# One of eight row blocks of the modulation weights multiplied on TensorE instead of VectorE

## The reference

```python
c_act = jax.nn.silu(c)                                    # (1, 1024)
mod = (c_act @ w_ada[i] + b_ada[i])[:, None, :]           # w_ada[i] is 1024 x 6144
sh1, sc1, g1, sh2, sc2, g2 = jnp.split(mod, 6, axis=-1)
h = rms_norm(x) * (1 + sc1) + sh1                         # x is (1, 1024, 1024)
proj = h @ w_in[i]
...
```

## Time and profile before

| | |
|---|---|
| time, median of 3 runs | 2814.91 us (2812.26 to 2815.58) |
| the profiled execution's own time | 2812.64 us |
| its span | 2810.8 us (1.84 us lie around it) |
| PE (TensorE) busy | 2741.2 us, 98% |
| DVE (VectorE) busy | 1631.8 us, 58% |
| ACT (ScalarE) busy | 956.0 us, 34% |
| POOL (GpSimd) busy | 942.9 us, 34% |
| PE share of the chain that ended last | 92% |

### The profile page before, as it was taken

One profiled execution on the slowest core, in us unless ns is written; L12 is line 12 of the kernel. 1 busy time (PEld: TensorE's weight loads), 2 busy tenths in 40 slices (PEclk: granted clock), 3 DMA queues, 4 the chain that ended last, 5 costly groups with the idle time before them and its releaser, 6 DMA issues.

```text
span 2810.8 us, 60971 instructions
## 1 busy us (share of the span) xinstructions
PE 2741.2 (98%) x25491; PEld 2287.8 (81%) x25491; DVE 1631.8 (58%) x1807; ACT 956.0 (34%) x1447; POOL 942.9 (34%) x691
## 2 busy tenths in 40 slices
PE   5999999999999999999999999999999999999999
PEld 4798989898989898988787777788888788888887
DVE  4645454545454545469694666466648643333896
ACT  5312121212121212135555768301113333334343
POOL 0403030303030303034343111233333477777443
PEclk9999999999999999999999999999999999999999
DMA  5202020202020202033332111366511133234353
GB/s 211 74 22 61 21 61 21 61 21 61 21 61 21 61 21 61 11 116 115 119 112 72 34 62 50 118 196 211 173 58 45 53 113 113 85 100 142 124 170 92
DMA packets 255359, 235.00 MB, mean 84 GB/s; under 512 B 24353, under 2 KB 213883, under 8 KB 255099
## 3 DMA queue, kind: packets, MB, share of 16 engines
q1 hardware_dynamic: 241632, 183.74, 21.7%
q10 hardware_dynamic: 13467, 47.31, 4.8%
HBM read 184.08 MB, written 46.92 MB: 82 GB/s over the span
## 4 chain that ended last, share of the span: by engine, by line
PE 92%; DVE 3%; ACT 2%; issue 1%; DMA 0%; SPq 0%; POOL 0%; ACTq 0%; DVEq 0%; POOLq 0%
PE ps L306 68%; PE ps L1243 3%; PE ps L1257 3%; PE ps L1254 2%; PE ps L1221 2%; PE ps L1306 1%; PE ps L1443 1%; PE ps L1468 1%; PE ps L1211 1%; PE ps L1456 1%; PE ps L1177 1%; PE ps L1263 1%; PE ps L1290 1%; PE ps L1280 1%; PE ps L1309 1%
## 5 line engine op out<-in xcount | busy, mean ns | idle before, releaser
L306 PE MATMUL ps<-x_hi,w_hi 128*128 128x512 f32 (+1 forms) x2372 | 801.4, 397 | 6.1 <-issue 2.0
L306 PE MATMUL ps<-x_hi,w_lo 128*128 128x512 f32 (+1 forms) x2372 | 783.2, 390 | 0.0
L306 PE MATMUL ps<-x_lo,w_hi 128*128 128x512 f32 (+1 forms) x2372 | 782.9, 390 | 0.0
L296 POOL CAST w_hi<-w_raw 128x1024 fp32r<-128x1024 f32 (+2 forms) x161 | 153.5, 954 | 1544.8 <-PE ps L306 1292.2
L306 PEld LDWEIGHTS ps<-x_hi,w_hi 128*128 128x128 f32 (+1 forms) x2372 | 436.8, 187 | 114.5 <-issue 22.4
L306 PEld LDWEIGHTS ps<-x_hi,w_lo 128*128 128x128 f32 (+1 forms) x2372 | 443.9, 187 | 96.8
L306 PEld LDWEIGHTS ps<-x_lo,w_hi 128*128 128x128 f32 (+1 forms) x2372 | 444.2, 187 | 92.6
L298 POOL TENSOR_TENSOR w_lo<-w_raw,w_hi 128x1024 fp32r<-128x1024 f32 (+2 forms) x161 | 329.3, 2045 | 12.9
L306 PE MATMUL ps<-x_sums,w_hi 128*128 128x512 f32 x648 | 201.7, 392 | 0.6 <-issue 0.6
L1054 POOL TENSOR_TENSOR w_lo<-arena,w_hi 128x384 fp32r<-128x384 f32 (+1 forms) x124 | 154.6, 1248 | 111.2 <-ACT w_hi L2216 111.2
L2519 DVE COPY_PREDICATED arena<-hid,ps 128x256 f32<-128x256 int32 x144 | 72.0, 500 | 139.4 <-PE ps L1254 88.6
(11 more groups left out here) (346 smaller groups left out, 4449.2 us busy)
## 6 DMA issues: line engine op xcount, KB each, us to landing
w_raw<-in_w_in SPq DMA_DIRECT2D x78, 512.0 KB, 3.9
arena<-in_w_ada SPq DMA_DIRECT2D x48, 512.0 KB, 5.8
arena<-gates_sig ACTq DMA_DIRECT2D x40, 512.0 KB, 4.3
w_raw<-in_w_ffn_in SPq DMA_DIRECT2D x26, 512.0 KB, 4.0
gates_sig<-arena ACTq DMA_DIRECT2D x24, 512.0 KB, 2.7
under<-in_w_ffn_in SPq DMA_DIRECT2D x18, 512.0 KB, 5.7
hidden_sums<-arena SPq DMA_DIRECT2D x36, 256.0 KB, 2.6
under<-hidden_sums SPq DMA_DIRECT2D x11, 768.0 KB, 5.8
```

The lines of the kernel that those rows point to most:

```text
L296: nc.gpsimd.tensor_copy(hi, raw).then_inc(s_whi, 1)
L306: ins = nc.tensor.matmul(dst[h], wp, xp[h], start=first and m == 0, stop=last and m == 2, skip_group_check=on)
```

## The change

Piece 4 no longer goes through VectorE. Before `mod_sums` of the first half, TensorE waits for silu(c) and for the part that holds piece 4, and multiplies it by eight matmuls: stationary operand 128 columns of the raw piece, moving operand the column of silu(c). They open the accumulation in columns 0 to 7 of bank 0 of `ps`, and the eight matmuls of `mod_sums(0, 0)` now add to what stands there (`start=False`). VectorE leaves piece 4 out; so that all later counts stay as they were, piece 5 waits for the count of 4 and raises `ada_acc` by two.

```diff
+        ADA_ON_PE = (4,)
...
             def mod_sums(half, bank):
                 pe.wait_ge(ada_acc, upto(KT if half == 0 else ADA_ACC0))
+                own = half > 0
                 for c in range(KT):
-                    ins = mm(ps[:, bank, c:c + 1], ada_acc0[:, half, c * P:(c + 1) * P], ones[:, 0:1], start=True, stop=True)
+                    ins = mm(ps[:, bank, c:c + 1], ada_acc0[:, half, c * P:(c + 1) * P], ones[:, 0:1], start=own, stop=True, skip_group_check=not own)
                 ins.then_inc(ada_pe, 1)
 
+            pe.wait_ge(p0_act, upto(1))
+            for n in ADA_ON_PE:
+                part, count = ada_part(n)
+                pe.wait_ge(s_ada[part], 16 * count)
+                for c in range(KT):
+                    mm(ps[:, 0, c:c + 1], ada_w0[:, n, c * P:(c + 1) * P], mod[:, 48 + n:49 + n], start=n == ADA_ON_PE[0] and c == 0, stop=False, skip_group_check=True)
             mod_sums(0, 0)
...
                 if n in first:
                     ins = v.tensor_scalar(acc, ada_w0[:, n % ADA_SLOTS, :], c_k, None, ALU.mult)
                 else:
-                    dve.wait_ge(ada_acc, upto(n))
+                    dve.wait_ge(ada_acc, upto(4 if n == 5 else n))
                     ins = v.scalar_tensor_tensor(acc, ada_w0[:, n % ADA_SLOTS, :], c_k, acc, ALU.mult, ALU.add)
-                ins.then_inc(ada_acc, 1)
+                ins.then_inc(ada_acc, 2 if n == 5 else 1)
...
             for n in range(2, KT):
-                ada_piece(n)
+                if n not in ADA_ON_PE:
+                    ada_piece(n)
```

## The result

The changed kernel takes 2819.55 us (median of 20 runs, 2815.59 to 2821.79), the kernel before 2813.67 us in as many runs beside it (2811.49 to 2815.92). The ratio is 1.0021, with a 95% interval of 1.0014 to 1.0027: **slower by 5.9 us**, outside the range of the prediction and on the side to which it gave a chance of 0.03. The profiled execution took 2818.98 us, its span is 2817.2.

A forecast was written before the change was run, and what follows sets the result against it. TensorE was taken as the bound, busy 98% of the span, so only an earlier first dense product counts: 0.11 us off for the removed multiplication, nothing for the added rows, from 2814.91 to 2814.8 us. Range 2811.5 to 2817.0.

The forecast's parts named there:

- The added work's price of nothing: Sixteen TensorE rows from about 25.6 us, in idle time ahead of the sums, cost nothing; 1.8 to 3.6 us uncovered.
- The removed multiplication: In the opening, VectorE without piece 4 waits 1.28 us for part (5,8), so one multiplication less gains 0.11 us.
- Rival A: In the opening, TensorE at its high clock for the sums, 1.84 us not 3.58; gain 0.33 us, 2814.6; chance 0.11.
- Rival B: In the opening, part (5,8) lands before 28.4, so the whole multiplication is gained: 1.0 to 1.4 us, 2813.6; chance 0.07.
- Rival C: TensorE's low clock reaches into the first dense products: about 2.8 us slower, 2817.6; chance 0.07.
- Rival D: Part (5,8) lands 0.11 us later, VectorE starts piece 5 as before: no gain, 2814.9; chance 0.72 together with the forecast.

The follow-up runs named there:

- padded by 223: The changed kernel plus 223 unused semaphore increments in TensorE's list, everything behind lying 256 slots later than in the kernel before: ratio 1.0035.
- place 207: Loop start at slot 207 of a 256-slot block: the changed kernel +5.9 us, kernel before plus only the added matmuls +5.5, plus only 33 increments +5.8.
- 174: Loop start at slot 174 of a 256-slot block, as in the kernel before; the changed kernel with its loop set there: ratio 0.9994, 2812.65 us.
- place 238: The kernel before plus 64 unused increments in TensorE's list, loop start at slot 238 of a 256-slot block: ratio 1.0057, +15.8 us.
- 14: The changed kernel with its loop set to start at slot 14 of a 256-slot block: ratio 1.0054, 2829.13 us.
- 142: The changed kernel with its loop set to start at slot 142 of a 256-slot block: ratio 1.0016, median 2820.21 us.
- the padding of 192: The kernel before plus 192 unused increments in TensorE's list, loop start at slot 110: ratio 1.0072, +21.1 us, 6 of it in the opening.

## Why the prediction was wrong

- **The step that failed** is in its first paragraph: "a change in the opening is worth what it moves the moment at which TensorE starts its dense products, and after that moment the program follows unchanged". The instructions are unchanged, their place isn't. The padded kernel, the same except for 33 empty slots, is 5.8 us slower, and the changed kernel with its loop in the old place is not slower.
- **The added work's price of nothing** missed the same term. Its sixteen rows did run in idle time, from 27.56 for 3.54 us. Their price was 33 slots of TensorE's list, and it is paid in the loop: 4.8 us by the table. No rival named it. The profile of before held a hint that I didn't follow: pauses of TensorE with no releaser. The waits view of the kernel before, over the loop:

```profile
PE ps L1290 <- issue: 5.0, 8, 0.9
PE ps L1263 <- issue: 0.9, 4, 0.3
```

  The hint says where to look and not how much it is worth: all such pauses in the loop add up to 6.3 us before and to 6.9 after, and the 5.0 us of the first row are 4.9 after. The rest of the loop's loss is in steps that the view doesn't name and in the half clock.

- **The removed multiplication** was sized right. The reading of the landings held: part (5,8) landed 4.0 us after piece 4 in the profile after, 4.06 by the estimate. From the first multiplication of part (2,5) to the first of part (5,8) it is 4.17 us before and 4.03 to 4.05 in four of six traces without piece 4 on VectorE (a seventh, padded by 223, starts so late that all its parts have landed), a gain of 0.12 to 0.14 us for the 0.11 forecast. In the other two the part landed later, and it is 4.51 and 5.03 (waits of 1.84 and 2.36 us): a loss of 0.3 and 0.9. So the term is right for the trace that it was read from and of no fixed sign beyond it. The gain can't be seen in any ratio; 0.9994 and 1.000 allow it and don't show it.
- **Rival A** fell: the sums took 3.58 us in the changed kernel too. **Rival B** fell: the wait was there in each trace of the change except the one padded by 223. **Rival C** had the right sign for a wrong reason: the first products ran at full pace, 12 rows in 3.02 us. **Rival D** can't be told from the forecast by the ratio; the two late landings are of its kind.
- **The range** was built of the spread of executions of one program. Three runs at one place of the loop could not contain what another place does.
- **The half clock** is a second term that the prediction had at nothing behind the opening. By the granted clock of each run (mean 0.99895 over the 20 of the changed kernel, 0.99926 over 31 of the kernel before) it is, as an estimate, 0.0003 x 2817 = 0.9 us of the 5.9. Whether the change has to do with it is not shown; the two runs with the place 207 and without the whole change have 0.99856 and 0.99873.

The Trainium skill, in "Runtime: NRT & Kernel Launch", section Instruction fetch mechanics, says that an engine's instructions come in blocks of 16 KiB, 256 instructions, that each is fetched while the one before is executed, and that crossing a boundary is mostly hidden. The traces agree on the block (packets of 16 KB, pauses some 125 matmuls or 250 slots and their waits apart). They differ on the hiding: among small matmuls, of which TensorE executes a block in 3.64 us, it pauses at block ends in every trace. The same section says that a taken branch to a block that isn't held must wait for it. At place 238 the wait of 0.72 us stands not at the branch's target but at the next block's start, 13 slots on; no run here isolates the branch.

**What stays open.** Why one place is good and another bad: my own rule for it failed at 14. It looks as if TensorE starts the small matmuls with some blocks in advance, loses a part of that with each block, and is dry earlier or later depending on the place; that is argued from the positions of the pauses (mainly from 1268 or 1283 at places 174 and 207, from 862 at 14), not shown. That the pauses are waits for the next block rests on their place and on their distance from the fetches, and no run changed the fetching itself. Nor is it shown why one place, 142, has two groups of times.

## What to carry to other kernels

An edit that adds or removes instructions ahead of a long stretch of short ones moves that stretch against the blocks in which it is fetched, and on this kernel that alone is worth up to 20 us of 2813 (the loop's time at places 174 and 238). Before a difference of a few tenths of a per cent is put down to the work, compare with a version that has only the shift, or put the loop in the same place in both. And before one pays for a shorter chain of work on data that is still landing, one asks for the landing of every piece, not only of the one that the chain names.

## What was not expected of the hardware

- TensorE pauses for its own instructions, as far as their place and the fetches tell: mostly 0.2 to 0.9 us, up to 1.2 us in the profile after and 1.8 with the padding of 192, some 125 matmuls apart, in a loop of some 4500 slots and 140 us a turn.
- An increment of a semaphore in TensorE's list takes 0.15 us in the opening: 112 of them fill the 16.7 us of idle time ahead of the added matmuls in the run with 223.
- TensorE can be granted half its clock for 3.4 us in the middle of work: at 492.8 us with 39 rows in the stretch, and at 2151.7 us in dense products of 128x512. Of the fourteen traces five have such a stretch between the opening and the last instruction.
